# Third attention of a two-block transformer: scores of the two components issued in turn, behind one wait for both score places

## The chip, the cores and the metric

The kernel runs on one core of a Trainium2 chip. The metric is the device time of one execution in microseconds (us). TensorE (PE in the profile) multiplies matrices; its weight loads have a row of their own, PEld. VectorE is DVE, ScalarE is ACT, SyncE (SP) issues the weight transfers.

## The reference

One function runs a two-layer block with context tokens and then a second block of another kind. The change lies in the odd layer of the first block, a differential attention: 512 latent and 256 context tokens as keys, 8 heads, and two components (t = 0, 1) of 64 dimensions in each head.

```python
def diff_attend(q, k, v, lam, lambda_init, subln_g):
    s = jnp.einsum('bqhtd,bkhtd->bthqk', q, k).astype(jnp.float32) * HEAD_DIM ** -0.5
    p = jax.nn.softmax(s, axis=-1)
    a = (p[:, 0] - lam * p[:, 1]).astype(v.dtype)
    o = jnp.einsum('bhqk,bkhe->bqhe', a, v)
    o = rms_norm(o, subln_g) * (1.0 - lambda_init)
    return o.reshape(o.shape[0], o.shape[1], DIFF_HEADS * 2 * HEAD_DIM)
```

## The kernel before, in words

The program is written engine by engine. Each engine has its own list of instructions, in an order set by hand, and the engines meet by semaphores. There is no planner: what an engine does next is the next line of its list.

The third attention works on 32 units (`DIFF_UNITS`), one for each head h and block i of 128 queries. A unit goes through these steps, each on the engine named:

- TensorE, `diff_score`: the scores of 128 queries with 768 keys, for t = 0 and then t = 1. Component t lies in partitions 64 t to 64 t + 63 of the queries and keys, so each of its matmuls uses 64 rows. `score_runs` cuts the keys into a run of 512 and a run of 256, so a unit has four matmuls in the code. In the trace each is a pair of records, a weight load and a matmul twice, so a unit shows eight.
- VectorE, L2883: the maximum of each component's scores, out of PSUM.
- ScalarE, L2036: the exponential of each component's scores, out of PSUM into SBUF, with the row sums in an accumulator that is read afterwards. The end of that read releases the component's place in PSUM (`psum_drained`).
- VectorE, L2898 to L2900: the two components are put together with the factor lambda and the row sums.
- TensorE, L1261: six transposes; ScalarE, L2045: a copy of the result into SBUF; TensorE: twelve records of the output with the values, added up for a head over its four blocks.

Each component has one place in PSUM, place t, of two banks. So unit n's component t can be written when unit n-1's exponential of component t is done. TensorE's list for step n of the main loop is: the scores of unit n, the transposes of unit n-2, the output of unit n-3, and after a head's last block a sum of squares over the head (eight small matmuls). VectorE's list for step n is the two maxima of unit n, then the combination of unit n-1, with a copy of a finished head's output (L2861) ahead of it once in four units. ScalarE's list is the two exponentials of unit n, then the copy of unit n-2, with the squares of a head (L2024) once in four.

The scores of unit 0 are issued ahead of the main loop, inside the last chunk of the value projection: component 0 after value tile t = 3, component 1 after t = 4, with six matmuls between and six behind. At step 4, ScalarE and VectorE also split a chunk of weights (L1716, L2317).

All matmuls of the kernel are issued through the helper `mm` (L675), so lines alone don't tell them apart; the tile names and shapes do. Score matmuls are those with `64*128` weights and 512 or 256 columns, out of `Y` (queries and keys lie in it).

Of the kernel before, what the change touches and what calls it, by code (L numbers as in the profile page):

```python
# [24 lines left out]
P = 128  # L25
# [7 lines left out]
HD = 64  # L33
# [145 lines left out]
def build(nc, io, known):  # L179
# [6 lines left out]
    with ExitStack() as ctx:  # L186
        def sb(name, shape, dt=F32):
# [26 lines left out]
        PS = [PSA[:, i, :] for i in range(PS_RING)] + [PSF[:, 3584:4096], PSF[:, 3072:3584],  # L214
                                                       PSF[:, 512:1024], PSF[:, 1536:2048],
                                                       PSF[:, 2560:3072]]
        PAIR_T = PSF[:, 2048:3584]

        def const(name, rows=slice(0, P)):
            a, n = C_AT[name]  # L220
            return C[rows, a:a + n]
# [5 lines left out]
        def sem(name):  # L227
            return ctx.enter_context(nc.semaphore(name))
# [54 lines left out]
        rope_done = sem("rope_done")  # L283
# [12 lines left out]
        psum_filled = [sem(f"psum_filled{i}") for i in range(len(PS))]  # L296
        psum_drained = [sem(f"psum_drained{i}") for i in range(len(PS))]
# [11 lines left out]
        def value(name, key=None):  # L309
            return known.get((name, key), 1)  # L310


        def take(key, at=None):

            if at is None:
                given["jobs"] = given.get("jobs", -1) + 1
                at = given["jobs"] % PS_RING
            given["slot", at] = given.get(("slot", at), 0) + 1
            known["job", key] = (at, given["slot", at])

        def slot(key):
            return known.get(("job", key), (0, 1))[0]

        def turn(key):
            return known.get(("job", key), (0, 1))[1]
# [8 lines left out]
        def w_last_job(key, *chunk):  # L334

            known["chunk", w_index[chunk]] = ("job", key)

        def last_use(*chunk):
            c = w_index[chunk]
            known["chunk", c] = ("used", c)  # L340
            return one("weights_used", c)
# [23 lines left out]
        def part(buf, at, *dims):  # L365
            n = int(np.prod(dims))
            v = buf[:, at:at + n]
            if len(dims) == 1:
                return v
            names = "abcd"[:len(dims)]  # L370
            return v.rearrange(f"p ({' '.join(names)}) -> p {' '.join(names)}",
                               **dict(zip(names, dims)))
# [55 lines left out]
        QD = part(Y, 0, DIFF_H, S)  # L428
        KDf = part(Y, DIFF_H * S, DIFF_H, T)
# [144 lines left out]
        DIFF_UNITS = [("diff", h, i) for h in range(DIFF_H) for i in range(4)]  # L574
# [5 lines left out]
        def head_at(n, lag):  # L580

            h = (n - lag) // 4
            return h if (n - lag) % 4 == 0 and 0 <= h < DIFF_H else None
# [45 lines left out]
        def score_runs(u):  # L629

            runs = []
            for c, (j, _) in enumerate(key_tiles(u)):
                if runs and runs[-1][1] + runs[-1][2] == j and c % 4:
                    runs[-1][2] += 1
                else:
                    runs.append([c, j, 1])
            return runs
# [35 lines left out]
        def _(pe):  # L673
            def mm(out, lhsT, rhs, first, last):
                return pe.matmul(out, lhsT, rhs, start=first, stop=last)  # L675
# [12 lines left out]
            def parts(chunk, cols=P):  # L688

                home = split_home(s_index[chunk])  # L690
                k = chunk_floats(chunk) // cols
                return home[:, :, 0:k * cols].rearrange("p a (k c) -> p a k c", c=cols)

            def products(out, w, x, first, last):

                mm(out, w[0], x[0], first, False)
                mm(out, w[0], x[1], False, False)
                return mm(out, w[1], x[0], False, last)
# [418 lines left out]
            for n in range(3, 9):  # L1117
                key, last = EVEN_JOBS[n], EVEN_JOBS[n - 1]
# [28 lines left out]
            for t in range(6):  # L1147
                ins = pe.transpose(PS[slot(("kr",))][0:96, t * P:(t + 1) * P], VS[:, t, HD:VR_N], const("ident"))
# [63 lines left out]
                    for at in (4, 5):  # L1212
                        pe.wait_ge(psum_drained[at], given["slot", at])

            def diff_score(u, n, t):
                _, h, i = u
                key = (u, "scores", t)
                take(key, t)
                if turn(key) > 1:
                    pe.wait_ge(psum_drained[slot(key)], turn(key) - 1)  # L1220
                r = slice(HD * t, HD * t + HD)
                for c, j, nj in score_runs(u):
                    ins = mm(PS[slot(key)][:, c * P:(c + nj) * P], QD[r, h, i * P:(i + 1) * P],
                             KDf[r, h, j * P:(j + nj) * P], True, True)
                ins.then_inc(psum_filled[slot(key)], 1)

            for g in range(2):
                for c in range(4):
                    chunk = ("diff_in", 16 + 4 * g + c)
                    pe.wait_ge(weights_split, s_index[chunk] + 1)  # L1230
                    w = parts(chunk, S)
                    for t in range(6):
                        key = ("dv", g, t // 2)
                        if c == 0 and t % 2 == 0:
                            take(key)
                            if turn(key) > 1:
                                pe.wait_ge(psum_drained[slot(key)], turn(key) - 1)
                        for k in range(2):
                            x = [HT2[:, a, 2 * c + k, t * P:(t + 1) * P] for a in range(2)]
                            ins = products(PS[slot(key)][:, (t % 2) * S:(t % 2 + 1) * S], x,  # L1240
                                           (w[:, 0, k], w[:, 1, k]), c + k == 0, c == 3 and k == 1)
                        if c == 3 and t % 2:
                            ins.then_inc(psum_filled[slot(key)], 1)
                        if g and c == 3 and t in (3, 4):
                            if t == 3:
                                for what in ("dq", "dk"):
                                    pe.wait_ge(rope_done, value("rope_done", (what, 7)))
                            diff_score(DIFF_UNITS[0], 0, t - 3)
                    if c < 3:
                        ins.then_inc(weights_used, last_use(*chunk))  # L1250
                    else:
                        w_last_job(("dv", g, 2), *chunk)

            def diff_transposes(u, n):
                key = (u, "turned")
                take(key, 2)
                if turn(key) > 1:
                    pe.wait_ge(psum_drained[slot(key)], turn(key) - 1)
                pe.wait_ge(rows_normalised, value("rows_normalised", u))
                for c in range(6):  # L1260
                    ins = pe.transpose(PS[slot(key)][:, c * P:(c + 1) * P], P0D[:, n % 3, c * P:(c + 1) * P],  # L1261
                                       const("ident"))
                ins.then_inc(psum_filled[slot(key)], 1)

            def diff_output(u, n):
                _, h, i = u
                key = ("head_out", h)
                if i == 0:
                    take(key, 4 + h % 2)
                    if turn(key) > 1:  # L1270
                        pe.wait_ge(psum_drained[slot(key)], turn(key) - 1)
                pe.wait_ge(psum_drained[slot((u, "turned"))], turn((u, "turned")))
                for j in range(6):
                    ins = mm(PS[slot(key)][:, i * P:(i + 1) * P], VD[:, j, h * P:(h + 1) * P],
                             diff_turned(n)[:, j // 2, (j % 2) * P:(j % 2 + 1) * P], j == 0, j == 5)
                if i == 3:
                    ins.then_inc(psum_filled[slot(key)], 1)
# [23 lines left out]
            units = DIFF_UNITS  # L1301
            pe.wait_ge(psum_drained[3], given["slot", 3])
            for n in range(len(units) + 5):
                if 1 <= n < len(units):
                    for t in range(2):
                        diff_score(units[n], n, t)
                if n == 3:
                    for g in range(2):
                        for j in range(3):
                            pe.wait_ge(psum_drained[slot(("dv", g, j))], turn(("dv", g, j)))  # L1310
                if 2 <= n < len(units) + 2:
                    diff_transposes(units[n - 2], n - 2)
                if 3 <= n < len(units) + 3:
                    diff_output(units[n - 3], n - 3)
                if head_at(n, 8) is not None:
                    head_sum(head_at(n, 8))
# [2094 lines left out]
```

## Time and profile before

| | |
|---|---|
| runs | 2805.75, 2805.91, 2811.44 us; median 2805.91 |
| span of the profiled execution | 2809.1 us (its own time isn't given beside it; the span is 3.2 us over the median) |
| mean granted TensorE clock | 0.988 |
| TensorE busy | 2725.6 us, 97% of the span |
| third attention, from the first score matmul to the last output | about 1267.6 to 1417.4 us |

The page shows one execution. Times in the rows are us from the start of the span. A timeline row gives start, duration, engine, line, operation, what is written from what, the shapes, and how many like instructions were merged; in brackets stands the idle time of the engine before it and what ended it. A row of windows gives the busy time of each engine in a stretch, the number of instructions, and the granted clock (PEclk, 1.00 is full).

### The profile page before, as it was taken

Reading aid. Unit: us, or ns where it says so; the run is one execution under the profiler, and the core shown is the slowest. Engines: PE = TensorE matmul, PEld = TensorE weight load, DVE = VectorE, ACT = ScalarE, POOL = GpSimd, SP = SyncE. Lnnn points to the kernel's source line nnn. Section 1 sums busy time; section 2 is a strip of 40 time slices with the busy share of each in tenths; the row PEclk is TensorE's granted clock in tenths of the full one; section 3 lists DMA queues with packets and bytes.
Section 4 is the critical chain, followed back from the end, with each engine's and each line's share of the span. In section 5 each row is a group of like instructions: output and inputs, shape, how many; then the busy total and the mean of one; then the engine's idle time right before and its main releaser. Section 6 shows DMA issues by size and latency. Waiting matters only on the chain.

```text
span 2809.1 us, 42633 instructions
## 1 busy us (share of the span) xinstructions
PE 2725.6 (97%) x18196; PEld 2250.0 (80%) x18196; DVE 1355.2 (48%) x2426; ACT 1014.7 (36%) x1635; POOL 66.6 (2%) x53
## 2 busy tenths in 40 slices
PE   7999999999999999999999999999988999999999
PEld 5876678888888887886788888888765888888887
DVE  3377544433233334426757646458658343533333
ACT  3355543322112224635635323342156222322221
POOL 2000000100000000000001000200000000000000
PEclk9999999999999999999999999999999999999999
DMA  6332010232333331210011332222220223222322
GB/s 260 105 114 76 24 38 31 76 113 103 119 109 105 108 103 39 81 63 16 1 61 61 102 104 95 85 82 74 86 80 9 92 96 98 91 90 84 106 90 88
DMA packets 67067, 235.66 MB, mean 84 GB/s; under 512 B 7360, under 2 KB 10560, under 8 KB 66240
## 3 DMA queue, kind: packets, MB, share of 16 engines
q1 hardware_dynamic: 66592, 231.38, 24.5%
q8 instruction: 144, 2.36, 0.3%
q10 hardware_dynamic: 288, 1.57, 0.2%
q14 instruction: 43, 0.35, 0.0%
HBM read 230.82 MB, written 2.10 MB: 83 GB/s over the span
## 4 chain that ended last, share of the span: by engine, by line
PE 90%; DVE 5%; ACT 2%; issue 1%; DMA 1%; SPq 0%; DVEq 0%; ACTq 0%
PE PSA L675 87%; PE PSA L990 2%; PE PSA L1261 1%; DVE stat L3148 1%; DMA Y<-in_early 1%; DVE WS L2317 1%; DVE Y L3139 0%; DVE HS L2493 0%; ACT WS L1716 0%; PE PSA L1615 0%; ACT Y L2178 0%; DVE PSA L3147 0%; DVE X L2431 0%; ACT HS L1803 0%; DVE YS L2317 0%
## 5 line engine op out<-in xcount | busy, mean ns | idle before, releaser
L675 PE MATMUL PSA<-HS,WS 128*128 128x512 f32 (+1 forms) x6480 | 1303.4, 361 | 11.6 <-DVE HS L2493 5.1
L675 PEld LDWEIGHTS PSA<-HS,WS 128*128 128x128 f32 x6480 | 1092.2, 189 | 211.7 <-issue 14.1
L2317 DVE TENSOR_TENSOR WS<-W,WS 128x1024 fp32r<-128x1024 f32 (+2 forms) x313 | 358.0, 1145 | 638.2 <-ACT WS L1716 637.6
L1716 ACT ACTIVATE WS<-W 128x1024 fp32r<-128x1024 f32 (+2 forms) x313 | 308.3, 986 | 756.9 <-PE PSA L675 383.5
L675 PE MATMUL PSA<-YS,WS 128*128 128x512 f32 (+1 forms) x2232 | 468.6, 371 | 3.6 <-DVE YS L3172 3.6
L675 PEld LDWEIGHTS PSA<-YS,WS 128*128 128x128 f32 x2232 | 391.4, 188 | 78.6 <-DVE YS L3172 4.0
L675 PE MATMUL PSA<-Y 128*64 128x128 f32 (+9 forms) x2368 | 286.2, 342 | 18.6 <-ACT Y L2178 6.7
L675 PEld LDWEIGHTS PSA<-Y 128*64 128x64 f32 (+3 forms) x2368 | 174.4, 151 | 97.5 <-issue 65.5
L675 PE MATMUL PSA<-HS,YS 128*128 128x512 f32 (+1 forms) x696 | 125.6, 337 | 0.4 <-DVE X L2424 0.4
L675 PEld LDWEIGHTS PSA<-HS,YS 128*128 128x128 f32 x696 | 106.6, 189 | 16.1 <-issue 2.3
L2640 DVE TENSOR_TENSOR Y<-Y,PSA 128x512 f32<-128x512 f32 (+1 forms) x66 | 51.2, 776 | 137.4 <-PE PSA L675 129.1
L1867 ACT ACTIVATE Y<-PSA,stat 128x768 f32<-128x768 f32 (+4 forms) x96 | 67.7, 706 | 100.9 <-DVE stat L2591 69.1
L675 PE MATMUL PSA<-WS,HS 128*128 128x512 f32 (+2 forms) x528 | 95.8, 342 | 0.2 <-DVE Y L3031 0.2
L675 PE MATMUL PSA<-YS,HS 128*128 128x256 f32 (+1 forms) x624 | 92.5, 303 | 2.4 <-DVE X L2387 1.2
L675 PEld LDWEIGHTS PSA<-WS,HS 128*128 128x128 f32 x528 | 82.6, 189 | 13.4 <-issue 1.9
L2612 DVE TENSOR_TENSOR YS<-Y,YS 128x512 fp32r<-128x512 f32 (+1 forms) x66 | 52.2, 791 | 82.3 <-ACT YS L1883 82.3
L1690 ACT ACTIVATE Y<-PSA 128x512 f32<-128x512 f32 (+4 forms) x67 | 45.3, 685 | 126.8 <-PE PSA L675 126.4
L675 PEld LDWEIGHTS PSA<-YS,HS 128*128 128x128 f32 x624 | 82.6, 190 | 9.0 <-issue 1.7
L2591 DVE TENSOR_REDUCE stat<-PSA 128x1 f32<-128x768 f32 (+4 forms) x96 | 67.9, 712 | 39.2 <-PE PSA L675 37.5
L1893 ACT ACTIVATE Y<-PSA,PR 128x768 f32<-128x768 f32 (+1 forms) x44 | 39.0, 886 | 127.2 <-PE PSA L675 127.2
L2622 DVE SCALAR_TENSOR_TENSOR Y<-PSA,PR,Y 128x511 f32<-128x511 f32 x66 | 41.6, 658 | 84.5 <-ACT Y L1893 84.3
L2036 ACT ACTIVATE Y<-PSA,stat 128x768 f32<-128x768 f32 x64 | 57.1, 896 | 56.1 <-DVE stat L2883 56.1
(348 smaller groups left out, 2271.1 us busy)
## 6 DMA issues: line engine op xcount, KB each, us to landing
W<-in_weights SPq DMA_DIRECT2D x391, 512.0 KB, 3.5
Y<-in_early SPq DMA_DIRECT2D x4, 2048.0 KB, 19.3
W<-in_weights SPq DMA_DIRECT2D x24, 256.0 KB, 2.7
X<-in_x SPq DMA_DIRECT2D x4, 768.0 KB, 20.7
W<-in_weights SPq DMA_DIRECT2D x24, 128.0 KB, 2.2
Y<-in_ssm ACTq DMA_DIRECT2D x1, 1024.0 KB, 7.2
out<-X SPq DMA_DIRECT2D x1, 1024.0 KB, 4.5
C<-in_consts SPq DMA_DIRECT2D x1, 884.5 KB, 31.0
```

Of the source, the lines that this page charges most:

```text
L675: return pe.matmul(out, lhsT, rhs, start=first, stop=last)
L990: ins = pe.transpose(PAIR_T[:, (nk * t + c) * P:(nk * t + c + 1) * P], rows[:, c * P:(c + 1) * P], const("ident"))
L1690: act.activation(dst, ps[rows, lo:lo + n], func, scale=scale).then_inc(psum_drained[slot(key)], 1)
L1716: act.activation(split_home(n)[:, 0, 0:f], W[:, c % W_RING, 0:f], ACT.Copy)\
L1867: act.activation(pair_rows(u, n, t)[:, 0:w], PS[slot(key)][:, 0:w], ACT.Exp, bias=top[:, t:t + 1], accum_out=sums[:, t:t + 1])\
L1893: act.activation(gc, ps[:, 0:n], ACT.Identity, scale=par("conv_w", f * 66 + 22 + m, 1), bias=par("conv_b", f * 22 + m, 1)).then_inc(gate_b ...
L2036: act.activation(dst, PS[slot(key)][:, 0:T], ACT.Exp, bias=top[:, t:t + 1], accum_out=total)\
L2317: tt(home[:, 1, 0:f], W[:, c % W_RING, 0:f], home[:, 0, 0:f].bitcast(F32), ALU.subtract)\
L2591: ins = dve.tensor_reduce(pair_stat(n)[0][:, t:t + 1], ps[:, 0:k], AX_X, ALU.max, negate=True)
L2612: tt(a[:, 1, m - ms[0], :], GC[:, m % 3, 0:n], a[:, 0, m - ms[0], :].bitcast(F32), ALU.subtract).then_inc(activated, one("activated", (f, m)))
L2622: ins = stt(gc[:, lo + 1:lo + nn], ps[:, lo:lo + nn - 1], par("conv_w", f * 66 + m, 1), gc[:, lo + 1:lo + nn], ALU.mult, ALU.add)
L2640: tt(gc[:, 0:n], gc[:, 0:n], ps[:, 0:n], ALU.mult).then_inc(psum_drained[slot(("up", f, m))], 1)
```

## The change

For each unit the waits for both score places now stand ahead of the first score matmul, and the four matmuls are issued run by run: keys 0 to 511 of component 0, then of component 1, then the last 256 keys of component 0, then of component 1. Each component still signals VectorE with its own last matmul. Both components of unit 0 are issued after value tile t = 4, where before component 0 came after t = 3; the wait for the rotations of queries and keys moves with them.

```diff
-            def diff_score(u, n, t):
+            def diff_scores(u, n):
                 _, h, i = u
-                key = (u, "scores", t)
-                take(key, t)
-                if turn(key) > 1:
-                    pe.wait_ge(psum_drained[slot(key)], turn(key) - 1)
-                r = slice(HD * t, HD * t + HD)
+                keys = [(u, "scores", t) for t in range(2)]
+                for t, key in enumerate(keys):
+                    take(key, t)
+                    if turn(key) > 1:
+                        pe.wait_ge(psum_drained[slot(key)], turn(key) - 1)
                 for c, j, nj in score_runs(u):
-                    ins = mm(PS[slot(key)][:, c * P:(c + nj) * P], QD[r, h, i * P:(i + 1) * P],
-                             KDf[r, h, j * P:(j + nj) * P], True, True)
-                ins.then_inc(psum_filled[slot(key)], 1)
+                    for t, key in enumerate(keys):
+                        r = slice(HD * t, HD * t + HD)
+                        ins = mm(PS[slot(key)][:, c * P:(c + nj) * P], QD[r, h, i * P:(i + 1) * P],
+                                 KDf[r, h, j * P:(j + nj) * P], True, True)
+                        if c + nj == 6:
+                            ins.then_inc(psum_filled[slot(key)], 1)
...
-                        if g and c == 3 and t in (3, 4):
-                            if t == 3:
-                                for what in ("dq", "dk"):
-                                    pe.wait_ge(rope_done, value("rope_done", (what, 7)))
-                            diff_score(DIFF_UNITS[0], 0, t - 3)
+                        if g and c == 3 and t == 4:
+                            for what in ("dq", "dk"):
+                                pe.wait_ge(rope_done, value("rope_done", (what, 7)))
+                            diff_scores(DIFF_UNITS[0], 0)
...
                 if 1 <= n < len(units):
-                    for t in range(2):
-                        diff_score(units[n], n, t)
+                    diff_scores(units[n], n)
```

## Rows read from the trace of the kernel before

**Rows 1.** The page: busy times, and the chain by engine.
```profile
PE 2725.6 (97%) x18196; PEld 2250.0 (80%) x18196; DVE 1355.2 (48%) x2426; ACT 1014.7 (36%) x1635; POOL 66.6 (2%) x53
...
PE 90%; DVE 5%; ACT 2%; issue 1%; DMA 1%; SPq 0%; DVEq 0%; ACTq 0%
```
**Rows 2.** Windows: from unit 6's scores to unit 31's.
```profile
1299.70:1405.80 106.10, 106.10 (x699) 79.23 (x698) 82.84 (x143) 66.78 (x131) 0.00 (x0) 1.00 0.00 1
```
**Rows 3.** Timeline of TensorE, units 13 to 17, scores and head sum.
```profile
1329.40 1.57 PE L675 MATMUL PSA<-Y 64*128 64x512 f32 x8
...
1333.04 2.42 PE L675 MATMUL PSA<-Y 64*128 64x512 f32 x8
...
1337.54 1.57 PE L675 MATMUL PSA<-Y 64*128 64x512 f32 x8
...
1341.18 2.42 PE L675 MATMUL PSA<-Y 64*128 64x512 f32 x8
...
1345.58 0.95 PE L675 MATMUL PSA<-C,Y 128*128 128x1 f32 x8
1346.46 0.71 PE L675 MATMUL PSA<-Y 64*128 64x512 f32 x2
```
**Rows 4.** Timeline of all engines, units 15 and 16.
```profile
1337.54 0.31 PEld L675 LDWEIGHTS PSA<-Y 64*128 64x128 f32 x4
...
1339.13 1.82 DVE L2883 TENSOR_REDUCE stat<-PSA 128x1 f32<-128x768 f32 x2 [0.69 <-PE PSA L675]
...
1340.12 0.90 ACT L2036 ACTIVATE Y<-PSA,stat 128x768 f32<-128x768 f32 x1 [1.92 <-DVE stat L2883]
...
1341.01 0.89 ACT L2036 ACTIVATE Y<-PSA,stat 128x768 f32<-128x768 f32 x1
...
1341.18 0.29 PEld L675 LDWEIGHTS PSA<-Y 64*128 64x128 f32 x2
...
1341.31 1.02 DVE L2900 SCALAR_TENSOR_TENSOR Y<-Y,stat 128x768 f32<-128x768 f32 x1
...
1341.79 0.20 ACT L2036 ACTIVATION_READ_ACCUMULATOR Y<-PSA,stat 128x1 f32 x1
...
1342.77 1.82 DVE L2883 TENSOR_REDUCE stat<-PSA 128x1 f32<-128x768 f32 x2 [0.44 <-PE PSA L675]
```
**Rows 5.** Timeline of TensorE's weight loads at 1342 us, unit 16.
```profile
1342.05 0.18 PEld L675 LDWEIGHTS PSA<-Y 64*128 64x128 f32 x1
```
**Rows 6.** Groups by line, same stretch as rows 2: busy, mean ns, idle before.
```profile
L2883 DVE TENSOR_REDUCE stat<-PSA 128x1 f32<-128x768 f32 x50 | 45.5, 952 | 19.2 <-PE PSA L675 19.2
```
**Rows 7.** Timeline of TensorE, start of the stage: units 0, 1 and 4.
```profile
1267.56 1.55 PE L675 MATMUL PSA<-Y 64*128 64x512 f32 x4
1269.05 1.65 PE L675 MATMUL PSA<-WS,HS 128*128 128x512 f32 x6
1270.63 1.55 PE L675 MATMUL PSA<-Y 64*128 64x512 f32 x4
...
1273.70 2.12 PE L675 MATMUL PSA<-Y 64*128 64x512 f32 x8
...
1287.76 1.67 PE L675 MATMUL PSA<-Y 64*128 64x512 f32 x8
```
**Rows 8.** Timeline of TensorE: the scores of units 6 and 31.
```profile
1299.70 1.57 PE L675 MATMUL PSA<-Y 64*128 64x512 f32 x8
...
1405.80 1.57 PE L675 MATMUL PSA<-Y 64*128 64x512 f32 x8
```
**Rows 9.** Timeline of ScalarE: unit 5's second accumulator.
```profile
1298.38 0.20 ACT L2036 ACTIVATION_READ_ACCUMULATOR Y<-PSA,stat 128x1 f32 x1
```
**Rows 10.** Windows: units 1 and 2, and the end of the stage.
```profile
1273.70:1278.90 5.20, 3.62 (x15) 1.98 (x15) 3.13 (x5) 3.29 (x7) 0.00 (x0) 1.00 0.00 0
1278.95:1285.70 6.75, 6.75 (x19) 3.75 (x18) 3.96 (x6) 2.68 (x5) 0.00 (x0) 0.50 0.00 0
1408.50:1418.80 10.30, 7.41 (x66) 7.03 (x64) 4.33 (x11) 5.23 (x9) 0.00 (x0) 1.00 0.01 2
```

## The prediction

> **What bounds the kernel now.** I read the page first: TensorE is busy 97% of the span and holds 90% of the chain that ended last [rows 1], so time is won or lost on its queue. Then the busy time of the third attention: from the start of unit 6's scores to the start of unit 31's, 25 units take 106.10 us, 4.24 each, with TensorE busy all the time at the full clock (granted 1.00, 2.4 GHz) and VectorE and ScalarE far from full [rows 2]. By that view the stage is bound by TensorE, and work that packs better there should pay.
>
> The timeline of TensorE says something finer. Scores of one unit (four matmuls in the code, eight in the trace) take 1.57 us in one unit and 2.42 us in the next, in turn, and starts are 3.64, 4.50, 3.64 and 5.28 us apart, over and over: 17.06 us for four units, 4.27 each [rows 3]. The 5.28 has the sum of a head's squares in it, eight small matmuls.
>
> The timeline of all engines shows why [rows 4]. In the unit that starts at 1337.54, four weight loads of both components are issued within 0.31 us and all eight matmuls are over in 1.57: **the two components already run side by side**, though the code issues all of component 0 first. In the unit at 1341.18 only two loads go out; the first load of component 1 comes at 1342.05 [rows 5], 0.06 us after ScalarE has read the accumulator of the previous unit's second exponential (1341.79 + 0.20). So component 1's place was not free. Component 0 had a lead of 0.87 us, and the 2.42 is 1.57 plus most of that lead. "Busy" hides a wait there.
>
> Both kinds of unit share one chain, from the start of component 0 to the release of component 1's place. For the unit at 1337.54, from [rows 4, 5]: 1.59 us to the first maximum (1339.13), 0.99 to the first exponential (1340.12), 0.89 to the second (1341.01), 0.98 to the end of its accumulator's read (1341.99), 0.06 to TensorE's load (1342.05): **4.51 us**. The unit at 1341.18 has its first maximum at 1342.77, again 1.59 after its start. The maxima keep their size through the stage, 50 at a mean of 952 ns, and they waited 19.2 us for TensorE [rows 6].
>
> So two things alternate now. After a unit that ran side by side, TensorE's own work is done in 3.64 us and component 0 of the next starts ahead of the release. That unit is long for TensorE, but its chain has started 0.87 us earlier, and so its release comes in time for the next.
>
> **The change part by part.** *Order of the eight matmuls.* The units at 1.57 us already overlap fully, so I cost the new order at nothing there: same matmuls, same loads, same two increments. In the long units the overlap comes now too, 2.42 to 1.57 as TensorE sees it, but it is no gain by itself: component 1 starts when its place is free, at the same moment as before, and ends 1.57 later instead of 1.55. Unknown is how evenly the array shares the two streams when they are issued alternately. From below, component 0 could finish sooner than now: at best as it does alone in unit 0, where its four records take 1.55 us [rows 7], so nothing worth counting. From above, no overlap at all puts off both ends; that is a rival below. I take the 1.57 of the units that pair now, the nearest row.
>
> The Trainium skill (TensorE: Matmul & The Clock Gate, Part 3, The mechanism) says that matmuls on different row groups overlap, and that all matmuls start and end strictly in order of issue. The trace bears out the first half and not the second: four loads in 0.31 us and 1.57 us for eight matmuls cannot come from component 1 starting behind component 0's last. By the rule every unit would now be serial and the alternation would be what brings the overlap; by the rows it is there already. By the rule the sum would be the faster rival's, by the rows it is the one below.
>
> *The wait.* Component 0's four matmul records now wait for component 1's place. Behind them on TensorE's queue stand the transposes of unit n-2, the outputs of n-3 and a head's sum; these stood behind component 1's wait before and so lose nothing. The wait for place 0 itself costs nothing: its exponential starts 0.89 us ahead of the other. What loses is component 0: its start moves back by 0.87 us in each long unit, and with it the first maximum, both exponentials and the release. Next late is the following unit's start. From then on no unit has a lead, and each follows the last by the whole chain: 4.51 us. TensorE's work fits in that: 3.64, and with a head's sum 5.28 - 0.87 = 4.41. VectorE's normalising of the unit before ends at 1341.31 + 1.02, 4.79 after the start [rows 4]; the transposes that need it come 4.51 + 1.50 = 6.01 after it, so it stays off the path. ScalarE's copies come behind the exponentials as now.
>
> 25 units at 4.51 are 112.75 us instead of 106.10: **+6.65 us**. Unit 31 starts as a unit that pairs in both kernels (1.57 us at 1405.80 [rows 8]); I cost what follows it at nothing, since the ends of its chain lie as they do now.
>
> *Start of the stage.* Both components of unit 0 now go behind the value tile t = 4. Before: 1.49 us of scores, 1.58 of tile, scores, 1.58 of tile, unit 1 at 1273.70 [rows 7]. After: one tile first, some 1.3 to 1.6 us, so both start near 1269.0, and unit 1 follows a chain later at 1273.5. The wait for the rotations comes six matmuls later; nothing waited for it. Then three chains, 13.5 us, bring unit 4 to 1287.0 against 1287.76. Units 4 to 6 hold the split of a weight chunk, which puts off unit 5's maxima; from unit 4's start to the release of unit 5's second place are 10.9 us (1298.58 + 0.06 - 1287.76, [rows 7, 9]). That is 1297.9, a gain of 1.8 us against 1299.70 [rows 8]: the lower end. Against it stands the clock. In units 1 to 3 TensorE will idle more than it does now, and it fell to half (1.2 GHz) here already, after 5.20 us with 3.62 busy [rows 10]. Scores that pair at half clock take some 1.4 us more and stand in the chain; once makes it 1299.3, and the 1.06 us by which TensorE came late to unit 6 (1299.70 against 1298.64) makes 1300.4, +0.7. A second unit at half clock makes +2.1: the upper end. I take nothing, between the two.
>
> Sum: +6.65, with 4.9 and 8.8 as ends. The profiled execution has a span of 2809.1 us, 3.2 over the median of the three runs, 2805.91; the difference goes on the median: 2805.9 + 6.7 = **2812.6 us**.
>
> **Rivals.**
> *A little slower, not measurably.* The chain comes out shorter than 4.51 because component 0 leads by some tenths inside the alternation, or the start gains its 1.8. At 4.27 a unit the steady part would be even, which needs 0.24 us. For it: nothing fixes how the array shares two streams. Against: with both places free, the two ends now lie within the 1.57. Time 2806 to 2810.8.
> *Faster: the order itself pays.* If TensorE's work were the period, three units in four would take 3.64 and one 4.41: 3.83 on average, 95.9 us for 25, 10.2 less than now: 2795.7. It needs the second place free within 3.64 us; from 4.27 on it pays. The rows give 4.51, and no part of the change shortens a maximum or an exponential. By the skill's rule on strict order (named above) this would be the outcome, since the overlap would be new.
> *Overlap lost.* If the streams take turns without overlapping, component 0 ends some 0.87 us later than in a pair (the long unit's 2.42 against 1.57 is the nearest price), and 25 chains grow to about 5.4: 2812.6 + 22 = 2834.
> *Half clock throughout.* About 0.9 us idle in each 4.51. Against: the 10.30 us at the end of the stage kept the full clock with 7.41 busy, 72% [rows 10], and the new loop has 3.64 of 4.51, 81%; the stretch that lost it had 70%, so the distance isn't large. If it fell in every unit, 1.4 us on 25 chains: 2848.
>
> **How the numbers follow.** The forecast, a period of 4.51, has 0.76; little slower 0.10; faster 0.06; overlap lost 0.05; half clock 0.03. A measurement of this kernel can tell about 0.2%, 5.6 us, from no change. The forecast's ends, 4.9 to 8.8, straddle that: 0.60 of its 0.76 lie above, 0.16 below. So slower 0.60 + 0.05 + 0.03 = 0.68, no change 0.16 + 0.10 = 0.26, faster 0.06. The range takes the forecast's ends (2810.8 to 2814.7), most of the little-slower case below, and about 2 us above for the spread of runs (2805.75 to 2811.44 before): 2806.5 to 2817.
>
> **What would show it.** Every unit's eight matmuls at about 1.57 us; starts 4.5 us apart in every unit, those with a head's sum too; TensorE idle some 0.9 us before each unit's first load, ended by ScalarE's second exponential (L2036); VectorE's wait for TensorE longer in sum; the stage from unit 6 to 31 near 112.8. Wrong would be: starts at 3.6 to 4.3 us (the chain is shorter than I read it), scores at 2.4 or more (no overlap), a first maximum well under 1.59 us after the unit's start, or half clock inside the steady part.

## The result, and the profile after

| kernel | median, us | against the kernel before on the same chips |
|---|---|---|
| before | 2808.47 (2805.66 to 2811.44, 6 runs) | |
| changed | 2816.85 (2814.17 to 2819.10, 6 runs) | 1.0028, 95% interval 1.0017 to 1.0039 |

The change makes the kernel 0.28% slower, 7.9 us by the ratio. The profiled execution has a span of 2816.0 us against 2809.1, 6.9 more. The forecast was +6.7 us, a time of 2812.6 us, with a range of 2806.5 to 2817; the measured time lies just under its upper end.

TensorE's timeline in the steady part of the changed kernel, units 15 to 18, answers to [rows 3]:

```profile
1341.51 1.56 PE L675 MATMUL PSA<-Y 64*128 64x512 f32 x8 [0.86 <-ACT Y L2037]
...
1346.08 1.56 PE L675 MATMUL PSA<-Y 64*128 64x512 f32 x8 [0.86 <-ACT Y L2037]
...
1349.62 0.95 PE L675 MATMUL PSA<-C,Y 128*128 128x1 f32 x8
1350.65 1.56 PE L675 MATMUL PSA<-Y 64*128 64x512 f32 x8
...
1355.23 1.56 PE L675 MATMUL PSA<-Y 64*128 64x512 f32 x8 [0.87 <-ACT Y L2037]
```

Every unit's scores take 1.56 us now, and every start here is 4.57 us behind the last. The turn of 3.64 and 4.50 is gone. The wait that was hidden inside a busy 2.42 is now an idle 0.86, ended by ScalarE's second exponential. Between 1346.08 and 1350.65 stands a head's sum, and the step is no longer: the sum lies in what would be idle.

The whole steady part in one row of windows, unit 6 to unit 31, answers to [rows 2]:

```profile
1300.33:1414.67 114.34, 97.37 (x700) 75.29 (x699) 83.05 (x143) 66.89 (x131) 0.00 (x0) 1.00 0.00 1
```

114.34 us instead of 106.10. TensorE is busy for 97.37 of them where it was busy throughout: the same work (700 and 699 matmul records) with idle time between. The groups by line in that stretch show the waits that grew, against [rows 6]; columns as there:

```profile
L2884 DVE TENSOR_REDUCE stat<-PSA 128x1 f32<-128x768 f32 x50 | 45.6, 953 | 30.1 <-PE PSA L675 30.1
...
L675 PE MATMUL PSA<-Y 64*128 64x512 f32 x101 | 28.9, 634 | 17.0 <-ACT Y L2037 16.5
```

VectorE's maxima wait 30.1 us for TensorE instead of 19.2, and TensorE's first score matmuls wait 16.5 us for the exponentials. TensorE waits for ScalarE, ScalarE for VectorE and VectorE for TensorE, in a ring; none is full.

The chain of one unit, from the timeline of all engines, answers to [rows 4, 5]:

```profile
1341.47 0.33 PEld L675 LDWEIGHTS PSA<-Y 64*128 64x128 f32 x4 [1.02 <-ACT Y L2037]
1341.51 1.56 PE L675 MATMUL PSA<-Y 64*128 64x512 f32 x8 [0.86 <-ACT Y L2037]
...
1343.07 1.82 DVE L2884 TENSOR_REDUCE stat<-PSA 128x1 f32<-128x768 f32 x2 [0.77 <-PE PSA L675]
...
1344.06 0.90 ACT L2037 ACTIVATE Y<-PSA,stat 128x768 f32<-128x768 f32 x1 [2.00 <-DVE stat L2884]
...
1344.95 0.89 ACT L2037 ACTIVATE Y<-PSA,stat 128x768 f32<-128x768 f32 x1
...
1345.73 0.20 ACT L2037 ACTIVATION_READ_ACCUMULATOR Y<-PSA,stat 128x1 f32 x1
1345.83 0.81 ACT L2046 ACTIVATE X<-PSA 128x768 f32<-128x768 f32 x1
1346.05 0.33 PEld L675 LDWEIGHTS PSA<-Y 64*128 64x128 f32 x4 [1.03 <-ACT Y L2037]
```

From load to load, 1341.47 to 1346.05: 1.60 us to the first maximum, 0.99 to the first exponential, 0.89 to the second, 0.98 to the end of its accumulator's read (1345.93), 0.12 to the next load. These are the parts read before, but for the last, which was 0.06.

### The profile page after: what moved, and what is told of

It reads as the page before. It is cut to its first block, busy times and chain, and to the rows that moved or that the text cites. A ratio compares the mean times of both kernels' runs of the same rounds, so it can differ in the third digit from the quotient of the medians.

```text
span 2816.0 us, 42664 instructions
## 1 busy us (share of the span) xinstructions
PE 2712.2 (96%) x18196; PEld 2243.9 (80%) x18196; DVE 1355.3 (48%) x2426; ACT 1014.4 (36%) x1635; POOL 66.5 (2%) x53
## 3 DMA queue, kind: packets, MB, share of 16 engines
q10 hardware_dynamic: 288, 1.57, 0.2%
## 4 chain that ended last, share of the span: by engine, by line
PE 88%; DVE 6%; ACT 4%; issue 1%; DMA 1%; SPq 0%; DVEq 0%; ACTq 0%
PE PSA L675 86%; ACT Y L2037 2%; PE PSA L990 2%; DVE stat L2884 1%; DVE stat L3149 1%; DMA Y<-in_early 1%; DVE WS L2318 1%; DVE Y L3140 0%; PE PSA L1616 0%; ACT WS L1717 0%; DVE HS L2494 0%; PE PSA L1263 0%; ACT Y L2179 0%; DVE PSA L3148 0%; ACT HS L1804 0%
## 5 line engine op out<-in xcount | busy, mean ns | idle before, releaser
L675 PE MATMUL PSA<-Y 128*64 128x128 f32 (+9 forms) x2368 | 269.2, 340 | 43.2 <-ACT Y L2037 24.4
L675 PEld LDWEIGHTS PSA<-Y 128*64 128x64 f32 (+3 forms) x2368 | 167.4, 150 | 115.2 <-issue 61.2
L1868 ACT ACTIVATE Y<-PSA,stat 128x768 f32<-128x768 f32 (+4 forms) x96 | 67.7, 706 | 100.8 <-DVE stat L2592 67.7
```

Source lines behind the costliest of these rows:

```text
L1868: act.activation(pair_rows(u, n, t)[:, 0:w], PS[slot(key)][:, 0:w], ACT.Exp, bias=top[:, t:t + 1], accum_out=sums[:, t:t + 1])\
```

## The experiments

The theory: a unit's chain from component 0's start to the release of component 1's place is a fixed 4.5 us; the wait ahead of component 0 takes away its lead, so every unit pays the whole chain; the order of the matmuls is neutral because TensorE pairs the two components by itself. The rival: the alternated order itself costs or gains. Stage times, one profiled execution for each kernel, are from the start of unit 6's scores to the start of unit 31's. Each ratio is to runs of the kernel before beside that kernel.

| kernel | stage, us | median, us | ratio to before, 95% interval |
|---|---|---|---|
| before | 106.10 | 2808.47 | |
| changed | 114.34 | 2816.85 | 1.0028, 1.0017 to 1.0039 |
| the wait alone | 114.32 | 2816.78 | 1.0027, 1.0019 to 1.0036 |
| the order alone | 106.75 | 2810.16 | 1.0006, 0.9996 to 1.0015 |
| waits swapped | 112.74 | 2817.34 | 1.0032, 1.0020 to 1.0044 |
| the start alone | 106.11 | 2806.74 | 0.9992, 0.9982 to 1.0002 |
| second bank | 98.19 | 2801.69 | 0.9975, 0.9965 to 0.9986 |
| short maxima, before | 98.48 | 2798.87 | 0.9960, 0.9944 to 0.9975 |
| short maxima, changed | 101.98 | 2800.24 | 0.9970, 0.9957 to 0.9982 |

The kernel before had a median of 2807.40 us beside the wait, the order, the swapped waits and the start, and of 2807.27 beside the last three.

**The wait alone.** Against the changed kernel:

```diff
-                for c, j, nj in score_runs(u):
-                    for t, key in enumerate(keys):
+                for t, key in enumerate(keys):
+                    for c, j, nj in score_runs(u):
```

> The wait alone: both score places waited for ahead of a unit's first score matmul, but the matmuls in the old order, all of component 0 and then all of component 1. If the wait is the cause and TensorE pairs the two components by itself: as the changed kernel, 0.2 to 0.35% over the kernel before, starts 4.5 to 4.6 us apart, scores 1.57 us. If the issue order matters (matmuls start strictly in order of issue): component 0 ends some 0.3 us sooner and component 1 only after about 2.8 us, so scores near 2.8 us and a period away from 4.57.

The same ratio as the change and the same stage to 0.02 us. TensorE's timeline of this kernel, two units:

```profile
1338.44 1.57 PE L675 MATMUL PSA<-Y 64*128 64x512 f32 x8 [0.86 <-ACT Y L2037]
...
1343.02 1.57 PE L675 MATMUL PSA<-Y 64*128 64x512 f32 x8 [0.86 <-ACT Y L2037]
```

All of component 0 is issued first here, and still the eight matmuls take 1.57 us. So the wait carries the whole effect, and the pairing is TensorE's own.

**The order alone.** Against the changed kernel:

```diff
-                for t, key in enumerate(keys):
-                    take(key, t)
-                    if turn(key) > 1:
-                        pe.wait_ge(psum_drained[slot(key)], turn(key) - 1)
                 for c, j, nj in score_runs(u):
                     for t, key in enumerate(keys):
+                        if c == 0:
+                            take(key, t)
+                            if turn(key) > 1:
+                                pe.wait_ge(psum_drained[slot(key)], turn(key) - 1)
```

> The order alone: matmuls alternated run by run, but component 1's place is waited for only ahead of component 1's own first matmul, so component 0's first run keeps its lead; its second run stands behind that wait. If the lead of component 0 is what counts: between the kernel before and the changed one, 0 to +4 us (0 to 0.15%), starts still alternating between about 3.6 and 4.5 to 4.9 us. If the alternation itself costs: as the changed kernel, +7 to +9 us, starts 4.5 to 4.6 us in every unit.

No measurable difference from the kernel before. Its timeline, five units (the window ends inside the last):

```profile
1338.94 2.02 PE L675 MATMUL PSA<-Y 64*128 64x512 f32 x8
...
1343.83 1.56 PE L675 MATMUL PSA<-Y 64*128 64x512 f32 x8
...
1347.46 2.43 PE L675 MATMUL PSA<-Y 64*128 64x512 f32 x8
...
1351.96 2.02 PE L675 MATMUL PSA<-Y 64*128 64x512 f32 x8
...
1356.06 1.16 PE L675 MATMUL PSA<-Y 64*128 64x512 f32 x3
```

Steps of 4.89 with a head's sum, then 3.63, 4.50 and 4.10: component 0 keeps a lead, and the stage is within 0.65 us of the kernel before. The rival falls with these two runs: the order does next to nothing, with the wait (114.34 against 114.32 us) or without it.

**Waits swapped.** The two waits of the changed kernel in the other order:

```diff
-                for t, key in enumerate(keys):
-                    take(key, t)
-                    if turn(key) > 1:
-                        pe.wait_ge(psum_drained[slot(key)], turn(key) - 1)
+                for t, key in enumerate(keys):
+                    take(key, t)
+                for key in reversed(keys):
+                    if turn(key) > 1:
+                        pe.wait_ge(psum_drained[slot(key)], turn(key) - 1)
```

> The changed kernel with its two waits in the other order, so that the place released last (component 1's) is waited for by the weight load itself and not by an instruction of its own ahead of it. If that instruction stands in the chain: period 4.51 instead of 4.57 us, the stretch from unit 6 to unit 31 near 112.8 instead of 114.3, 1.5 to 2 us less than the changed kernel. If it is hidden: no difference.

In the stage it came out as expected: starts 4.51 us apart, 112.74 us, 1.6 less. TensorE's timeline, two units, and then one row of ScalarE and one of TensorE's loads in this kernel:

```profile
1345.79 1.56 PE L675 MATMUL PSA<-Y 64*128 64x512 f32 x8
...
1350.30 1.56 PE L675 MATMUL PSA<-Y 64*128 64x512 f32 x8 [0.80 <-ACT Y L2038]
```

```profile
1350.04 0.20 ACT L2038 ACTIVATION_READ_ACCUMULATOR Y<-PSA,stat 128x1 f32 x1
...
1350.29 0.30 PEld L675 LDWEIGHTS PSA<-Y 64*128 64x128 f32 x4 [0.99 <-ACT Y L2038]
```

From the end of the read (1350.24) to the load are 0.05 us, near the 0.06 of the kernel before. In the changed kernel there are 0.12, and an instruction of its own stands there; by its line in that trace:

```profile
L1221 PEldq EVENT_SEMAPHORE  x33: 51/51/51, 1266.1 to 1414.6; - x33
```

It takes 51 ns each time, after the release. The whole time doesn't show the 1.6 us: the ratios, 1.0032 and 1.0028, lie inside each other's intervals, and the profiled spans, 2814.1 and 2816.0, are one execution each. In these two executions what follows unit 31's start took 1405.2 us here and 1401.3 in the changed kernel, so differences outside the stage are larger than 1.6 us.

**The start alone.** The kernel before with only unit 0 moved:

```diff
-                        if g and c == 3 and t in (3, 4):
-                            if t == 3:
-                                for what in ("dq", "dk"):
-                                    pe.wait_ge(rope_done, value("rope_done", (what, 7)))
-                            diff_score(DIFF_UNITS[0], 0, t - 3)
+                        if g and c == 3 and t == 4:
+                            for what in ("dq", "dk"):
+                                pe.wait_ge(rope_done, value("rope_done", (what, 7)))
+                            for half in range(2):
+                                diff_score(DIFF_UNITS[0], 0, half)
```

> The kernel before with only the start changed: both components of unit 0 behind value tile t = 4, in the old order and with the old waits. If the steady part holds the whole effect: within 2 us of the kernel before, unit 6 reached between 1.8 us sooner and 1 us later, units 6 to 31 in 106 us. If the start matters for what follows: 3 us or more over it.

Steady part as before, 106.11 us. TensorE's timeline, units 2, 3 and 6:

```profile
1275.59 2.44 PE L675 MATMUL PSA<-Y 64*128 64x512 f32 x8 [1.32 <-ACT Y L2036]
...
1279.22 2.44 PE L675 MATMUL PSA<-Y 64*128 64x512 f32 x8 [0.38 <-ACT Y L2036]
...
1295.61 1.57 PE L675 MATMUL PSA<-Y 64*128 64x512 f32 x8
```

Unit 6 came 4.1 us sooner in the profile, more than I expected. In this execution units 2 and 3 kept the full clock (granted 1.00 from 1275.59 to 1283.73), where the kernel before was granted 0.50 from 1278.95 to 1285.70 [rows 10]. The whole time doesn't bear that out beyond its interval, 0.9982 to 1.0002, so whether the earlier pair is worth anything stays open.

**A second bank for component 1.** This takes away what the wait waits for. From unit 5 on component 1's rows lie in two adjoining places of 768 columns that take turns (columns 1024 to 1791 and 1792 to 2559, so the middle one of three banks holds the end of one and the start of the other). Its first run of 512 keys has a bank of its own in each place; only its last run shares a bank with the unit before:

```diff
+        def diff_place(n, t):
+            at = 0 if t == 0 else 1792 if n >= 5 and n % 2 else 1024
+            return PSF[:, at:at + T]
...
+                early = turn(keys[1]) - (2 if n >= 5 else 1)
+                if early > 0:
+                    pe.wait_ge(psum_drained[1], early)
...
+                for t, (j, nj), last in ((0, first, False), (1, other[0], False), (0, rest, True), (1, other[1], True)):
+                    if t and last and n >= 5:
+                        pe.wait_ge(psum_drained[1], turn(keys[1]) - 1)
```

The transposes move to columns 2560 to 3327, the heads' outputs use one bank, and a head's sum is formed in the bank that is idle, ahead of the output instead of behind it (`head_variance` on VectorE accordingly one step earlier). These moves make room for the bank; no run took them alone.

> Takes the cause of the wait away: component 1's first run of 512 keys gets a second bank and alternates between two, so that of a unit's four matmuls only component 1's last run (256 keys) waits for the previous unit's second exponential. The bank comes from the heads' outputs (one bank instead of two) and the head sums move into the bank that is idle. If the place of component 1 sets the period: starts 3.6 to 3.7 us apart and about 4.4 with a head's sum, units 6 to 31 in 96 to 100 us against 106.1 before and 114.3 changed, 6 to 10 us (0.2 to 0.35%) less than the kernel before. If something else holds the period (the order, VectorE, ScalarE): no less than the kernel before.

0.25% faster than the kernel before, with the stage at 98.19 us. TensorE's timeline, four units, and then its loads in the second unit of a pair:

```profile
1340.77 1.56 PE L682 MATMUL PSA<-Y 64*128 64x512 f32 x8
...
1344.40 1.57 PE L682 MATMUL PSA<-Y 64*128 64x512 f32 x8
...
1348.13 1.56 PE L682 MATMUL PSA<-Y 64*128 64x512 f32 x8
...
1351.77 1.57 PE L682 MATMUL PSA<-Y 64*128 64x512 f32 x8
```
```profile
1336.15 0.30 PEld L682 LDWEIGHTS PSA<-Y 64*128 64x128 f32 x4
1336.69 0.19 PEld L682 LDWEIGHTS PSA<-Y 64*128 64x128 f32 x1 [0.24 <-issue]
1337.03 0.29 PEld L682 LDWEIGHTS PSA<-Y 64*128 64x128 f32 x3 [0.15 <-ACT Y L2056]
```

Steps of 3.63, 3.73 and 3.64, and 4.62 where a head's sum lies between, from 1336.15 to 1340.77. Each unit pairs and none waits 0.87 us; the second exponential now ends a wait of only 0.15 us, for the last run. So waiting for component 1's place was what held the period, and this version beats both kernels.

**Short maxima.** The same edit in the kernel before and in the changed one: each maximum is taken over P = 128 keys instead of T = 768, which leaves out part of the maximum.

```diff
-    dve.tensor_reduce(diff_stat(n)[0][:, t:t + 1], PS[slot(key)][:, 0:T], AX_X, ALU.max,
+    dve.tensor_reduce(diff_stat(n)[0][:, t:t + 1], PS[slot(key)][:, 0:P], AX_X, ALU.max,
```

> The kernel before with each maximum taken over 128 of the 768 keys (this leaves out part of the maximum), which cuts some 0.67 us out of the chain from scores to release and changes nothing on TensorE. If the chain and TensorE's work alternate as read: starts 3.64, 3.84, 3.64 and 4.6 us, units 6 to 31 in about 98.4 us, 7 to 8 us less than the kernel before. If TensorE alone bounds it, as its busy time says: no change.

> The changed kernel with the same short maxima (part of the maximum left out). If each of its units waits for the whole chain: starts 3.90 us apart, 4.42 with a head's sum, units 6 to 31 in about 100.8 us, 5 to 6 us less than the kernel before and 13 less than the changed kernel; the two short kernels some 2.4 us apart instead of 8.2. If the alternation itself costs: the two short kernels still some 8 us apart.

TensorE does the same work in these two as in their originals. The kernel before drops to 98.48 us in the stage (expected 98.4) and the changed one to 101.98 (expected 100.8); they lie 3.5 apart instead of 8.2. In the whole time the two can't be told apart: their intervals overlap. TensorE's timelines, first of the kernel before with short maxima, then of the changed one:

```profile
1337.64 1.57 PE L675 MATMUL PSA<-Y 64*128 64x512 f32 x8
...
1341.28 1.76 PE L675 MATMUL PSA<-Y 64*128 64x512 f32 x8
```
```profile
1344.80 1.56 PE L675 MATMUL PSA<-Y 64*128 64x512 f32 x8 [0.23 <-ACT Y L2037]
1348.71 1.56 PE L675 MATMUL PSA<-Y 64*128 64x512 f32 x8 [0.20 <-ACT Y L2037]
```

With 0.66 us off the chain the long unit shrinks from 2.42 to 1.76, and the wait of the changed kernel from 0.86 to 0.2. The stage that showed TensorE busy for all of its 106 us got 7.6 us shorter by an edit on VectorE alone. Of the 3.5 us between the two I had expected 2.4. Most of the rest is the step from unit 6 to unit 7, which began at half clock in both (granted 0.50 for its first 2.0 us in the changed one and 0.9 in the other): 4.93 us against 4.06.

## Why the prediction was right

**The pairing.** Right, and shown: the components overlap without the alternation (the wait alone), and the alternation without the wait changes nothing that can be measured in the whole time (the order alone). No unit bears out the faster rival.

**The wait takes the lead away and every unit pays the chain.** Right in kind, and shown from both sides: the wait alone gives the whole effect, a second bank takes it away, and a chain shorter by 0.66 us takes more than half of it away (3.5 of 8.2 us are left).

**The period, 4.51 us.** This term was mis-sized: 4.57. "The wait for place 0 itself costs nothing" was the step that failed. It is free as a wait, but two waits ahead of one load make an instruction of their own of one of them, here of the wait for component 1's place, which is released last. With the waits swapped the period is 4.51. Over 25 units this is 1.6 us, which is why the steady part grew by 8.24 and not by 6.65.

**A head's sum hidden.** Right: the one in the timeline of units 15 to 18 ends at 1350.57 (1349.62 + 0.95), 0.08 us ahead of the next unit.

**The start.** Costed at nothing, between -1.8 and +2.1: unit 6 starts at 1300.33 instead of 1299.70, +0.6. These are one execution each, and the wait-alone kernel, whose start is the same but for the order of the matmuls, had unit 6 at 1297.29 in its own; so the 0.6 is not shown to be the change's. As foreseen one unit's scores fell into half clock. TensorE's timeline of the changed kernel, units 2 and 3:

```profile
1278.23 1.56 PE L675 MATMUL PSA<-Y 64*128 64x512 f32 x8 [3.08 <-ACT Y L2037]
...
1282.80 2.64 PE L675 MATMUL PSA<-Y 64*128 64x512 f32 x8 [2.21 <-ACT Y L2037]
```

The price costed for it, some 1.4 us, was near: in the wait-alone kernel a unit wholly at half clock took 2.94 us, 1.37 more than its others. Here only part of the unit fell into it.

**What follows the stage.** Costed at nothing. In these two executions +0.6 and +8.2 make 8.9, and the span grew by 6.9, so 2 us came back behind the stage: from unit 31's start to the end of the span 1403.3 us before and 1401.3 after. Single executions differ by more than that. In the nine profiles of this document this part took 1399.7 (short maxima, changed) to 1405.2 us (waits swapped), so the 2 us are not shown to come from the change. Where most of them lie can be read. TensorE's timeline of the kernel before, at the first tiles of the next projection:

```profile
1420.88 2.53 PE L675 MATMUL PSA<-C,stat 128*128 128x128 f32 x16 [0.97 <-DVE stat L2902]
1424.36 4.18 PE L675 MATMUL PSA<-HS,WS 128*128 128x512 f32 x9 [0.95 <-DVE HS L2906]
...
1429.52 2.33 PE L675 MATMUL PSA<-HS,WS 128*128 128x512 f32 x9
```

The first nine matmuls ran at half clock here (granted 0.50 from 1424.36 to 1428.34). In the changed kernel the half clock came earlier, from 1429.90 to 1433.30 on the sixteen small matmuls, and had ended by the nine. The same piece after:

```profile
1429.72 3.63 PE L675 MATMUL PSA<-C,stat 128*128 128x128 f32 x16 [0.97 <-DVE stat L2903]
1433.96 2.29 PE L675 MATMUL PSA<-HS,WS 128*128 128x512 f32 x9 [0.61 <-DVE HS L2907]
...
1436.90 2.32 PE L675 MATMUL PSA<-HS,WS 128*128 128x512 f32 x9
```

The nine take 1.9 us less and the sixteen 1.1 more. From unit 31's start to the second nine are 23.72 us before and 22.23 after, 1.5 of the 2 us. No experiment aimed at this.

**The number.** That the span grew by 6.9 us, so near the forecast 6.7, is luck of these two executions: 1.6 us too little in the steady part and 2 too much behind it nearly cancel. The ratio gives +7.9 with an interval from 4.8 to 11.0, which holds both the forecast and the 8.2 of the stage: the 1.6 us are shown by the stage alone. The time of 2816.85 is 4.25 us over the forecast 2812.6. Of these 2.6 are the base, 2805.91 from three runs of the kernel before where six gave 2808.47, and the rest is the size of the change. Two small figures of the prediction are off without changing what they are used for: 25 units at 3.83 are 95.8 us, not 95.9, and the steady part is even at 4.24 us a unit, not at 4.27, which is the mean of four units and not of the 25.

**The other rivals.** The full clock was granted from unit 6 to unit 31, with TensorE 85% busy (97.37 of 114.34), so half clock did not come in the steady part. Overlap lost and little slower didn't come either.

## What to carry to other kernels

An engine that shows 100% busy may be waiting inside an instruction group: here a group that took 1.57 us in one turn and 2.42 in the next, with the same work, held a wait, and the chain through the other engines was the thing to add up. Before putting a second wait ahead of work that had one, ask whose chain starts with that work; a lead of 0.87 us on one half of it was worth some 0.3 us in every unit here (4.24 to 4.57). Where the place was what the work waited for, a second bank for part of it was worth 7.9 us in the stage (98.19 against 106.10), and the order of issue nothing that could be measured.

## What the runs showed of the hardware that I had not expected

- Two waits ahead of one weight load: one became an instruction of 51 ns in TensorE's queue, and it was the one issued second. Issuing the wait that is released last first put it on the load itself and made the handoff 0.05 us instead of 0.12.
- In the order-alone kernel, by its record, component 0's last matmul is over about 1.58 us after the unit's start (1347.46), but VectorE's maximum starts only 2.05 after it. The record that ends just before that is one of component 1's, issued earlier. That record, and the maximum:

```profile
1348.87 0.59 PE L675 MATMUL PSA<-Y 64*128 64x512 f32 x1
...
1349.51 1.82 DVE L2884 TENSOR_REDUCE stat<-PSA 128x1 f32<-128x768 f32 x2 [0.89 <-PE PSA L675]
```

The record ends at 1349.46, and the maximum begins 0.05 later. That looks as if matmuls of two row groups start out of order but signal in the order of issue. The Trainium skill (TensorE: Matmul & The Clock Gate, Part 3, The mechanism) has them strictly in order at both ends. The signal here (1349.51) agrees with that for the end; the starts do not, and neither do the ends in the records, which the profile models. No run was made to settle it.
